# Norm sums on all partitions, router work inside the last output projection, and a first expert pair without an empty result

## The chip, the cores and the metric

The kernel runs on one core of a Trainium2 chip. The metric is the device time of one execution in microseconds (us), taken as the median of several runs. TensorE (PE) multiplies matrices, VectorE (DVE) and ScalarE (ACT) do elementwise work, GpSimd (POOL) does a few small things, and SyncE (SP) starts the DMA transfers of the weights. PE's clock is granted at one of two levels, 1.2 GHz (0.5 in the profile) or 2.4 GHz (1.0).

## The reference

Two layers work on 272 tokens of width 1024 (16 learned meta tokens and 256 of input). Each layer adds a mixer of two halves, latent attention with 8 heads and a gated linear recurrence, and then a feed-forward. Layer 0 has a dense one, layer 1 a mixture of eight experts, two for each token.

```python
u = rmsnorm(h, norm_mix_g[l]);  proj = u @ w_in[l]
mix = concatenate([rmsnorm(att, attn_out_g[l]), rmsnorm(rnn, rnn_out_g[l])])
h = h + mix @ w_out[l]
u = rmsnorm(h, norm_ffn_g[l])
# layer 1: mixture of experts
logits = u @ router_w;  top_val, top_idx = top_k(logits, 2);  top_w = softmax(top_val)
out = sum over e of (gates[:, e:e+1] * (silu(u @ w_g[e]) * (u @ w_u[e]))) @ w_d[e]
```

`rmsnorm(x, g)` is `x / sqrt(mean(x*x) + 1e-6) * g`.

## The kernel before

The hidden state `hT` lies with its 1024 features on partitions, as 8 chunks of 128 features by 272 tokens. Weights come over one queue of SP into a ring of four slots (`raw`). ACT copies each piece to fp32r (`whi`, L843), DVE subtracts the copy from the original (`wlo`, L1206), and PE multiplies each product three times (`matmul3`, L585 to L587: high by high, low by high, high by low). The rings `whi` and `wlo` have four slots, so ACT can copy piece s only when PE is done with piece s-4. All four engines run their own instruction streams in the order written and meet at semaphores. The eight PSUM banks are handed out by `plan_blocks`; `filled` counts blocks that PE has finished, and `emptied` counts for each bank how often its reader is done.

**Norms.** For the first norm of a layer (`n1ss`), `sums` (L1745) adds the squares into one row of 272. ACT takes the root of that row into `rr` (`root_rows`, L875, followed by a tiny `mark`, L811), DVE takes the reciprocal (`rows`, L1218), PE spreads the row over 128 partitions (`spread`, L1750, block `n1bc`), and ACT copies the result to `rsb` (L855). DVE then scales every block of the input projection by `rsb` (L1264). The norm of the recurrence (`rnss`, `rnbc`) goes the same way, except that DVE reads the spread sums from PSUM (`rn_scaled`, L1418). In PE's order `rnbc` stands after the turned attention output of tile 1 (L1954) and ahead of the values of tile 2 (L1930, L1943), and both `rnbc` and that output use bank 4.

**Last output projection (layer 1).** PE first does the recurrence's half (12 matmuls a block) of blocks 0 to 3 while the attention ends. Then it turns the last attention tile (L1954), ACT writes its high part (L1015), DVE its low part (L1409), and PE does the attention half of blocks 0 to 3 (12 matmuls each) and all 24 matmuls of blocks 4 to 7. For each block DVE adds to `hT` (L1476) and writes `u32`, which is `hT` by the gain (L1481), and ACT squares `hT` into `qT` (L865).

**Router.** PE then adds the squares of the tokens by 16 matmuls with one moving column (L1998, block `n2ss`), computes the logits by 16 matmuls with eight moving columns (L2059, `lg`), and turns `u32` (blocks `ut`) and `hT` (blocks `ht`), each 16 chunks, to tokens on partitions (L2069). DVE scales the logits, picks the best two (L1565 to L1570), asks ACT for an exponential (L1097), and works out `sel` and `gate` in a chain of small operations (L1572 to L1584). ACT and DVE write the tokens as high and low parts, `uhi` (L1103) and `ulo` (L1593). PE counts the places of the tokens (`cum`, L2076 to L2080), DVE writes one-hot matrices for the first pair of experts (`hot`, L1621), and PE gathers the pair's tokens by multiplying with them (L2107, 16 matmuls of the high and 16 of the low part), which ACT copies to `xeh` and `xel` (L1117).

**Experts.** `expert` handles one expert: `hidden` (L2149) in 16 pieces, `turn` (L2161), `down` (L2174) in 8. The result of an expert is copied out of PSUM at the start of the next (`result`: L1123, L1641), scattered back by `combine` (L2122, L2123), and added to `acc` by `add_expert` (L1635). The first expert thus combines an empty result: `onehT` and column 0 of `gate` are zero. A loop takes six experts as three pairs, and the last two are written out.

Of the kernel before, what the change touches and what calls it, by code (L numbers as in the profile page):

```python
# [138 lines left out]
class Chain:  # L139
# [11 lines left out]
    def loop(self, times, per):  # L151
        start = self.base + self.n
        with self.eng.Fori(0, times) as i:
# [22 lines left out]
              ("out", 1), ("rnbc", None), ("values", 2), ("out", 2)],  # L176
             [("scores", 1), ("scores", 2), ("values", 1), ("rnss", None), ("out", 1), ("rnbc", None), ("values", 2),
# [8 lines left out]
def plan_blocks():  # L186
# [6 lines left out]
    for l in range(DEPTH):  # L193
        def add(*name, bank=None):
            pl.add((l, *name), bank)
        for k, (n, c) in enumerate(IN_BLOCKS[:N_IN - CH]):
# [3 lines left out]
            if k == 2:  # L200
                add("n1bc", bank=4)
# [38 lines left out]
        for m in range(KD):  # L240
            add("wo", m)
        if l == 0:
            for j, b in enumerate((0, 1, 2, 3)):
                pl.add(("ff0", j), b)
            pl.loop("ff", [4, 5, 6, 7, 0, 1, 2, 3], 5)
            pl.loop("dn", [4, 5, 6, 7], 2)

        else:
            add("n2ss", bank=4)
            pl.add("lg", 0)  # L250
            for n in ("ut", "ht"):
                for t in range(2):
                    for hf in range(2):
                        pl.add((n, t, hf))
            pl.add("cum", 4)
# [33 lines left out]
for _l in range(DEPTH):  # L289
    for _name in ["n1", "lat", "qk", "rnn"]:  # L290
# [4 lines left out]
def build(nc, ins, out):  # L295
# [4 lines left out]
    with ExitStack() as ctx:  # L300
# [92 lines left out]
        lgt = sb("lgt", [P, 2, NE], to=moe)  # L393
        top = sb("top", [P, 2, 8], to=moe)
# [70 lines left out]
        n2_root = sem("n2_root")  # L465
        qscale_done = sem("qscale_done")
# [18 lines left out]
        topx = sem("topx")  # L485
        sel_done = sem("sel_done")
# [226 lines left out]
        def _(pool):  # L713
# [63 lines left out]
            for l in range(DEPTH):  # L777
# [18 lines left out]
                if l:  # L796
                    power(rv[:, 3:5])
# [5 lines left out]
        def _(act):  # L803
# [63 lines left out]
            def broadcast(b):  # L867

                take(b, rsb[:, :])
                mark().then_inc(rsb_done, 1)  # L870
# [38 lines left out]
            for l in range(DEPTH):  # L909
# [6 lines left out]
                root_rows(B[l, "n1ss"], 1)  # L916
                for k, (name, c) in enumerate(IN_BLOCKS[:N_IN - CH]):
                    if k == 2:
                        broadcast(B[l, "n1bc"])
# [104 lines left out]
                for k0, t in enumerate(tl):  # L1024
# [16 lines left out]
                    if t == 2:  # L1041
                        root_rows(B[l, "rnss"], 1)
# [55 lines left out]
            for t in range(2):  # L1098
                for hf in range(2):
                    b = B["ut", t, hf]  # L1100
                    act.wait_ge(filled, b.ready())
                    act.wait_ge(rstd_done, POWERS[1, "n2"])
                    act.activation(uhi[:, :, :].rearrange("p k t -> p (k t)")[:, t * D + hf * 512:t * D + hf * 512 + 512],  # L1103
                                   ps[:, b.bank, :], ACT.Copy, scale=rv[:, t + 3:t + 4]).then_inc(tok_hi, 1)
            for t in range(2):
                for hf in range(2):
                    take(B["ht", t, hf], acc[:, t, hf * 512:hf * 512 + 512], cols=slice(0, 512))

            def experts(p):
                e0 = NE * p  # L1110
                base = [(XB[b] * NE + 2) * p for b in range(2)]
# [13 lines left out]
                def expert(e, gathers, more):  # L1125
# [16 lines left out]
                    result(used)  # L1142
                    w(e, p, 3, 4, 5, 6)
                    sigmoid(0, HALF_A // 2)
                    w(e, p, 7, 8, 9, 10, 11, 12, 13, 14)
# [21 lines left out]
                with act.Fori(0, PAIRS - 1) as i:  # L1167
                    expert(2 * i, None, True)
                    expert(2 * i + 1, i + 1, True)
# [17 lines left out]
        def _(dve):  # L1187
# [62 lines left out]
            for l in range(DEPTH):  # L1250
# [3 lines left out]
                rows(l, "n1", 1)  # L1254
# [159 lines left out]
                def rn_scaled(cs):  # L1414
                    b = B[l, "rnbc"]
                    dve.wait_ge(filled, b.ready())
                    for c in cs:
                        dve.scalar_tensor_tensor(tb[:, c, c0:T], xc[:, c, c0:T], col("rnn_out_g", l, c),  # L1418
                                                 bank(b, cols=slice(c0, T)), ALU.mult, ALU.mult).then_inc(rg_done, 1)
# [36 lines left out]
                rows(l, "rnn", 1)  # L1456
                normed(1)
                out_low(1)
                for h in range(0, NH, 2):
# [3 lines left out]
                    if h == 2:  # L1463
                        dve.engine_nop().then_inc(emptied[B[l, "rnbc"].bank], 1)
# [83 lines left out]
            w(0, 0, 0, 1, 2)  # L1548
# [711 lines left out]
```

## Time and profile before

| | us |
|---|---|
| median of 3 runs | 1068.51 |
| lowest, highest | 1061.14, 1069.38 |
| the profiled execution | 1068.87 |
| its span in the trace | 1067.1 |

The profiled execution lies 1.8 us above its span, which is time outside the first and last recorded instruction. Times in rows are us from the start of the span. The first number of a row is where the piece starts, the second how long it is.

### The profile page before, as it was taken

How to read it: one execution, taken by the hardware profiler on the slowest of the kernel's cores; microseconds unless marked ns; L12 is line 12 of the kernel's file. 1: busy time of each engine (PE TensorE's matmuls, PEld its weight loads, DVE VectorE, ACT ScalarE, POOL GpSimd, SP SyncE). 2: the span in 40 equal slices, each digit the busy share in tenths (PEclk: the TensorE clock that was granted, in tenths of full speed). 3: DMA queues.
4: the chain of work that ended last, by engine and by line, in shares of the span. 5: the costliest groups of instructions: out<-in, count | busy, mean ns of one | idle time of the engine just before them, and what ended most of it. 6: DMA issues, size and time to landing. Idle time of an engine off the chain costs nothing.

```text
span 1067.1 us, 15698 instructions
## 1 busy us (share of the span) xinstructions
PE 982.7 (92%) x5858; PEld 863.2 (81%) x5858; DVE 729.6 (68%) x967; ACT 573.5 (54%) x769; POOL 37.5 (4%) x67
## 2 busy tenths in 40 slices
PE   5997977999999999997967889999999999999995
PEld 3973644899999999873655889898989898989893
DVE  5554565556666555554564458897989798979893
ACT  4464053445444443453161347778777877687771
POOL 4130010000000000000000000000000000000000
PEclk9988865899999999998875969999999999999998
DMA  8401302145557673401311316998999899989971
GB/s 258 160 8 37 115 2 79 61 152 184 160 191 204 163 213 90 163 1 39 119 51 68 119 50 229 354 338 307 350 361 324 315 354 343 336 314 341 358 286 42
DMA packets 120019, 203.76 MB, mean 191 GB/s; under 512 B 5875, under 2 KB 73741, under 8 KB 119965
## 3 DMA queue, kind: packets, MB, share of 16 engines
q1 hardware_dynamic: 119504, 202.81, 55.3%
q8 instruction: 34, 0.56, 0.2%
q10 hardware_dynamic: 460, 0.23, 0.1%
q14 instruction: 21, 0.16, 0.0%
HBM read 201.98 MB, written 1.05 MB: 190 GB/s over the span
## 4 chain that ended last, share of the span: by engine, by line
PE 82%; DVE 9%; ACT 4%; issue 2%; DMA 0%; ACTq 0%; DVEq 0%; POOL 0%; POOLq 0%
PE ps L2149 20%; PE ps L585 11%; PE ps L2174 11%; PE ps L587 10%; PE ps L586 10%; PE ps L1745 3%; DVE wlo L1206 3%; PE ps L1820 2%; PE ps L2107 2%; ACT whi L843 1%; PE ps L1868 1%; PE ps L1750 1%; PE ps L1851 1%; PE ps L1943 1%; PE ps L1939 1%
## 5 line engine op out<-in xcount | busy, mean ns | idle before, releaser
L1206 DVE TENSOR_TENSOR wlo<-raw,whi 128x1536 fp32r<-128x1536 f32 (+4 forms) x296 | 437.5, 1508 | 91.7 <-ACT whi L843 89.7
L843 ACT ACTIVATE whi<-raw 128x1536 fp32r<-128x1536 f32 (+4 forms) x296 | 376.7, 1286 | 167.8 <-PE ps L587 88.2
L585 PE MATMUL ps<-uhi,whi 128*128 128x272 f32 (+1 forms) x576 | 172.6, 300 | 2.9 <-DVE ulo L1224 2.9
L587 PE MATMUL ps<-uhi,wlo 128*128 128x272 f32 (+1 forms) x576 | 170.4, 296 | 0.0
L586 PE MATMUL ps<-ulo,whi 128*128 128x272 f32 (+1 forms) x576 | 170.2, 295 | 0.0
L2149 PE MATMUL ps<-whi,xeh 128*128 128x320 f32 (+1 forms) x512 | 124.7, 325 | 0.0
L2149 PE MATMUL ps<-whi,xel 128*128 128x320 f32 (+1 forms) x512 | 123.6, 323 | 0.0
L2149 PE MATMUL ps<-wlo,xeh 128*128 128x320 f32 (+1 forms) x512 | 123.5, 323 | 0.0
L585 PEld LDWEIGHTS ps<-uhi,whi 128*128 128x128 f32 (+1 forms) x576 | 112.7, 196 | 9.6 <-issue 9.1
L586 PEld LDWEIGHTS ps<-ulo,whi 128*128 128x128 f32 (+1 forms) x576 | 113.1, 196 | 0.0
L587 PEld LDWEIGHTS ps<-uhi,wlo 128*128 128x128 f32 (+1 forms) x576 | 112.7, 196 | 0.0
L2149 PEld LDWEIGHTS ps<-whi,xeh 128*128 128x128 f32 x512 | 88.9, 188 | 1.9
L2149 PEld LDWEIGHTS ps<-whi,xel 128*128 128x128 f32 x512 | 89.1, 188 | 0.0
L2149 PEld LDWEIGHTS ps<-wlo,xeh 128*128 128x128 f32 x512 | 89.1, 188 | 0.0
L2174 PE MATMUL ps<-whi,heh 128*128 128x512 f32 x176 | 70.0, 398 | 0.0
L2174 PE MATMUL ps<-wlo,heh 128*128 128x512 f32 x176 | 69.6, 395 | 0.0
L2174 PE MATMUL ps<-whi,hel 128*128 128x512 f32 x176 | 69.5, 395 | 0.0
L587 PE MATMUL ps<-ahi,wlo 128*128 128x272 f32 x176 | 50.9, 289 | 0.0
L585 PE MATMUL ps<-ahi,whi 128*128 128x272 f32 x176 | 50.7, 288 | 0.0
L586 PE MATMUL ps<-alo,whi 128*128 128x272 f32 x176 | 50.6, 287 | 0.0
L2174 PEld LDWEIGHTS ps<-whi,hel 128*128 128x128 f32 x176 | 33.1, 188 | 8.0
L2174 PEld LDWEIGHTS ps<-whi,heh 128*128 128x128 f32 x176 | 33.1, 188 | 7.1
(285 smaller groups left out, 1393.9 us busy)
## 6 DMA issues: line engine op xcount, KB each, us to landing
raw<-in_moe_w_down_dram SPq DMA_DIRECT2D x24, 1536.0 KB, 7.7
raw<-in_moe_w_gate_dram SPq DMA_DIRECT2D x16, 1536.0 KB, 7.7
raw<-in_moe_w_up_dram SPq DMA_DIRECT2D x16, 1536.0 KB, 8.1
raw<-in_moe_w_gate_dram SPq DMA_DIRECT2D x16, 1280.0 KB, 7.0
raw<-in_moe_w_up_dram SPq DMA_DIRECT2D x16, 1280.0 KB, 6.1
raw<-in_ffn_w_gate_dram SPq DMA_DIRECT2D x11, 1024.0 KB, 5.3
raw<-in_ffn_w_up_dram SPq DMA_DIRECT2D x11, 1024.0 KB, 5.3
raw<-in_ffn_w_down_dram SPq DMA_DIRECT2D x8, 1408.0 KB, 7.0
```

What stands on the lines that cost most here:

```text
L585: pe.matmul(dst, wh, xh, start=start, stop=False, skip_group_check=True)
L586: pe.matmul(dst, wh, xl, start=False, stop=False, skip_group_check=True)
L587: return pe.matmul(dst, wl, xh, start=False, stop=stop, skip_group_check=True)
L843: act.activation(placed(whi, s, src), src, ACT.Copy).then_inc(hi_done, 1)
L1206: dve.tensor_tensor(placed(wlo, s, src), src, placed(whi, s, src).bitcast(F32), ALU.subtract).then_inc(lo_done, 1)
L1745: q = pe.matmul(ps[0:n, bk, 0:T], con[r, at:at + n], src(c)[r, :], start=(i == 0), stop=(i == len(parts) - 1))
L1750: return pe.matmul(ps[0:width, bk, 0:T], ident[0:rows, row:row + 1].to_broadcast([rows, width]), rr[0:rows, :], start=True, stop=True)
L1820: q = pe.matmul(bank(b, slice(0, QKH)), wq[:, k, h * QKH:(h + 1) * QKH], cq[:, k, :], start=(k == 0), stop=(k == QC - 1))
L1851: q = pe.matmul(bank(b, slice(0, NOPE)), wkv[:, k, at:at + NOPE], ckv[:, k, :], start=(k == 0), stop=(k == KVC - 1))
L2107: m = pe.matmul(ps[:, b, c * 2 * P:(c + 1) * 2 * P], part[:, t * D + at:t * D + at + P], onehot[:, t, :, :], start=(t == 0), stop=(t == 1))
L2149: q = pe.matmul(ps[:, 2 * kind + n, 0:width], xs[:, kk, half, :], w[:, sl, at:at + width], start=(kk == 0 and xs is xeh and w is whi), sto ...
L2174: q = pe.matmul(ps[:, 4 + n, :], xs[:, kk, :], w[:, sl, at:at + 512], start=(kk == 0 and xs is heh and w is whi), stop=(kk == FEC - 1 and ...
```

## The change

1. **Norm sums.** A new helper `total` sums with a stationary matrix of ones, so that the sum of squares stands on all 128 partitions. ACT takes its root straight into `rsb` (for `n1`) or `rr` (for `rnn`), and DVE takes the reciprocal there. The blocks `n1bc` and `rnbc` with their spread matmuls are gone, and so is ACT's copy to `rsb`.
2. **Last output projection of layer 1.** Its blocks use three banks in turn, with the recurrence's half of three blocks (0 to 2) done ahead, not of four. After block m, PE runs `chosen(m-1)`: one matmul of the logits with the router weights stationary and 256 tokens moving, and the two turns of `u32` for that chunk. POOL adds the squares of chunks 1 to 6 to chunk 0, so that `n2ss` takes 4 matmuls. The logits stand on 8 partitions: ACT copies them, and PE turns them by two small transposes.
3. **Router.** The best two are picked from logits that are not scaled. `sel` comes from one comparison and one addition, the exponential and `gate` come later, in the first expert (`shares`). ACT copies weight piece 0 ahead of `uhi` and pieces 1 and 2 behind it. DVE takes the low part of piece 0 ahead of `pos` and `hot`, writes `ulo` behind `hot`, and takes pieces 1 and 2 after that.
4. **First expert.** It has no `result`, no `combine` and no `add_expert`. The turns of `hT` and their copies to `acc` are done inside it instead. The first pair is written out in front of the loop, which now takes two pairs.

```diff
-                root_rows(B[l, "n1ss"], 1)
+                root_all(B[l, "n1ss"], rsb[:, :], D, n1_root)
-                    if k == 2:
-                        broadcast(B[l, "n1bc"])
...
+            def root_all(b, dst, n, done):
+                act.wait_ge(filled, b.ready())
+                act.activation(dst, bank(b), ACT.Sqrt, bias=eps[:, :], scale=1.0 / n).then_inc(emptied[b.bank], 1)
+                act.wait_ge(emptied[b.bank], b.before + 1)
+                mark().then_inc(done, 1)
...
+            def total(bk, src, n):
+                for c in range(n):
+                    q = pe.matmul(ps[:, bk, 0:T], ones(slice(0, P), P), src[:, c, :], start=(c == 0), stop=(c == n - 1))
+                return q
...
 # POOL
                 if l:
+                    for m in range(1, KD - 1):
+                        pool.wait_ge(nsq_done, 3 * KD + m + 1)
+                        pool.tensor_tensor(qT[:, 0, NMETA:T], qT[:, 0, NMETA:T], qT[:, m, NMETA:T], ALU.add)\
+                            .then_inc(nsum_done, 1)
+                        pool.wait_ge(nsum_done, m)
                     power(rv[:, 3:5])
...
 # PE, last projection and router
-                halves = range(4)
+                halves = range(4 if l == 0 else 3)
+                def chosen(c):
+                    b = B["lgT"]
+                    pe.wait_ge(u_done, c + 1)
+                    q = pe.matmul(ps[0:NE, b.bank, 0:SEQ], rw[:, c, :], u32[:, c, NMETA:T], start=(c == 0), stop=(c == KD - 1))
+                    for t in range(2):
+                        b = B["ut", t, c // 4]
+                        lead, n = TILES[t + 1]
+                        q = pe.transpose(ps[:, b.bank, c % 4 * P:c % 4 * P + P], u32[:, c, lead:lead + n], ident)
...
+                    if l and m:
+                        chosen(m - 1)
+                    chosen(KD - 1)
+                        for c in (0, KD - 1):
+                            q = pe.matmul(ps[:, b.bank, t:t + 1], qT[:, c, lead:lead + n], one[:, :], start=(c == 0),
+                                          stop=(c == KD - 1))
+                    for t in range(2):
+                        q = pe.transpose(ps[:, b.bank, t * NE:(t + 1) * NE], rr[0:NE, t * P:(t + 1) * P], ident[0:NE, 0:NE])
...
 # ACT
-            w(0, 0, 0, 1, 2)
-            act.wait_ge(top_done, 1)
-            act.activation(rtmp[:, 1, 0:2], rtmp[:, 0, 0:2], ACT.Exp).then_inc(topx, 1)
+            act.activation(rr[0:NE, 0:SEQ], ps[0:NE, b.bank, 0:SEQ], ACT.Copy).then_inc(emptied[b.bank], 1)
+            mark().then_inc(lgs_done, 1)
+            w(0, 0, 0)
...             # the four uhi (L1103)
+            w(0, 0, 1, 2)
...
                     w(e, p, 3, 4, 5, 6)
                     sigmoid(0, HALF_A // 2)
+                    if first and not p:
+                        act.activation(rtmp[:, 1, 0:2], rtmp[:, 0, 0:2], ACT.Exp).then_inc(topx, 1)
+                        for t in range(2):
+                            for hf in range(2):
+                                take(B["ht", t, hf], acc[:, t, hf * 512:hf * 512 + 512], cols=slice(0, 512))
...
 # DVE
+            link(dve.tensor_tensor(pick[:, :, :, :], e8, chosen, ALU.is_equal))
+            dve.tensor_tensor(sel[:, :, 0:NE], pick[:, :, 0, :], pick[:, :, 1, :], ALU.add).then_inc(sel_done, 1)
+            w(0, 0, 0)
...             # pos, hot(0, 0), the four ulo (L1593)
+            w(0, 0, 1, 2)
...
-                    result((NE + 1) * p + e + 1)
+                    if not first:
+                        result(NE * p + e)
                     w(e, p, 3, 4, 5, 6)
                     silu(0, HALF_A // 2)
+                    if first and not p:
+                        shares()
+                    if not first:
+                        add_expert(0, [n0[0] + 1, n0[1] + 1], e)
...
 # every engine
-                    expert(2 * i, 0, i, None)
-                    expert(2 * i + 1, 1, i, i + 1)
+                expert(0, 0, 0, None, True)
+                expert(1, 1, 0, 1)
+                with pe.Fori(0, PAIRS - 2) as i:
+                    expert(2 * i + 2, 0, i + 1, None)
+                    expert(2 * i + 3, 1, i + 1, i + 2)
```

## Rows read from the trace of the kernel before

**Rows 1.** The page, part 1: busy time of each engine over the span.

```profile
PE 982.7 (92%) x5858; PEld 863.2 (81%) x5858; DVE 729.6 (68%) x967; ACT 573.5 (54%) x769; POOL 37.5 (4%) x67
```

**Rows 2.** The chain that ended last, 590 to 712 us: start, length, what.

```profile
593.73 0.39 PE ps L585
...
610.98 0.13 PE ps L587
...
612.12 6.22 PE ps L1998 x32
618.34 6.85 PE ps L2059 x32
...
630.62 1.31 PE ps L2069 x8
...
636.38 5.54 PE ps L2107 x32
641.92 8.36 PE ps L2149 x48
650.28 0.23 PE ps L2122
```

**Rows 3.** Windows: busy time of PE, PEld, DVE, ACT, POOL; PE clock; DMA share; GB/s.

```profile
612.00:613.00 1.00, 0.88 (x8) 0.88 (x8) 0.00 (x0) 1.00 (x2) 0.00 (x0) 1.00 0.00 0
...
638.00:639.00 1.00, 1.00 (x7) 1.00 (x6) 0.00 (x0) 0.71 (x2) 0.00 (x0) 0.50 0.00 0
```

**Rows 4.** Timeline, recurrence norm, layer 1; in brackets idle time before, and releaser.

```profile
570.00 1.13 DVE L1409 SCALAR_TENSOR_TENSOR mx<-ps,vec,mx 128x128 fp32r<-128x128 f32 x4 [2.07 <-ACT mx L1015]
...
571.17 1.27 PE L1750 MATMUL ps<-rr,con 1*128 1x272 f32 x2 [2.47 <-DVE mx L1409]
...
573.10 0.42 DVE L1369 COPY pT<-ps 128x256 f32<-128x256 f32 x1 [1.98 <-PE ps L1930]
```

**Rows 5.** Timeline, the same place in layer 0.

```profile
178.50 0.42 DVE L1369 COPY pT<-ps 128x256 f32<-128x256 f32 x1 [1.98 <-PE ps L1930]
```

**Rows 6.** Timeline of PE around the spread of the first norm, layer 0.

```profile
33.14 0.72 PE L1750 MATMUL ps<-rr,con 1*128 1x272 f32 x2
33.79 0.39 PE L585 MATMUL ps<-uhi,whi 128*128 128x272 f32 x1
```

**Rows 7.** Timeline of DVE, last projection and router.

```profile
586.96 0.49 DVE L1392 TENSOR_SCALAR osb<-osb,rv 128x512 f32<-128x512 f32 x1 [0.73 <-POOL rv L755]
...
595.45 0.42 DVE L1476 TENSOR_TENSOR hT<-hT,ps 128x256 f32<-128x256 f32 x1 [1.79 <-PE ps L587]
...
613.48 5.09 DVE L1206 TENSOR_TENSOR wlo<-raw,whi 128x1536 fp32r<-128x1536 f32 x3 [1.52 <-ACT whi L843]
...
625.80 0.23 DVE L1565 MAX8 top<-lgt 128x8 f32<-128x8 f32 x2
...
635.12 1.11 DVE L1621 TENSOR_SCALAR onehot<-con,pos,sel 128x128 fp32r<-128x128 f32 x4
```

**Rows 8.** Timeline of ACT, router.

```profile
616.21 1.28 ACT L1097 ACT_TABLE_LOAD   x1
...
628.73 0.69 ACT L1103 ACTIVATE uhi<-ps,rv 128x512 fp32r<-128x512 f32 x1 [0.17 <-PE ps L2069]
...
631.31 2.57 ACT L855 ACTIVATE acc<-ps 128x512 f32<-128x512 f32 x4 [1.04 <-PE ps L2069]
```

**Rows 9.** Timeline of POOL: one operation at 22 us, and one in layer 1.

```profile
22.40 1.74 POOL L739 TENSOR_SCALAR rope<-rope 32x272 f32<-32x272 f32 x1
...
503.69 1.80 POOL L786 TENSOR_TENSOR vt<-vt,con 128x512 f32<-128x512 f32 x1 [40.34 <-ACT vt L855]
```

**Rows 10.** Timeline of PE, sums of squares in layer 1's first norm.

```profile
424.52 3.83 PE L1745 MATMUL ps<-u,con 128*1 128x272 f32 x16
```

**Rows 11.** Windows of two experts, number 4 in the loop, number 6 behind it.

```profile
848.12:898.09 49.97, 49.61 (x281) 45.95 (x280) 46.50 (x39) 36.46 (x32) 0.00 (x0) 1.00 0.95 353
...
951.21:1001.17 49.96, 49.60 (x280) 45.93 (x280) 46.44 (x39) 36.38 (x32) 0.00 (x0) 1.00 0.95 354
```

More of the change, by code:

```diff
@@ L240, in plan_blocks @@
         for m in range(KD):
-            add("wo", m)
+            add("wo", m, bank=None if l == 0 else m % 3)
+            if l and m == 4:
+                pl.add(("ut", 0, 0), 4)
+                pl.add(("ut", 1, 0), 6)
         if l == 0:
@@ L248, in plan_blocks @@
         else:
[L249 to L255, printed above, removed]
+            pl.add("lgT", 3)
+            pl.add(("ut", 0, 1), 5)
+            pl.add(("ut", 1, 1), 7)
+            add("n2ss", bank=2)
+            pl.add("lg", 3)
+            pl.add("cum", 3)
+            for t in range(2):
+                for hf in range(2):
+                    pl.add(("ht", t, hf), 4 + 2 * t + hf)
     return pl
@@ L289 @@
 for _l in range(DEPTH):
-    for _name in ["n1", "lat", "qk", "rnn"]:
+    for _name in ["lat", "qk"]:
         ROWS_DONE[_l, _name] = len(ROWS_DONE) + 1
@@ L1253, in _ @@
                     mix(l, 2, 3)
-                rows(l, "n1", 1)
+                dve.wait_ge(n1_root, l + 1)
+                dve.reciprocal(rsb[:, :], rsb[:, :]).then_inc(rsb_done, 1)
                 dve.wait_ge(rsb_done, 2 * l + 1)
@@ new lines, in _ @@
+            dve.wait_ge(emptied[b.bank], b.before + 1)
+            for t in range(2):
+                q = dve.max(top[:, t, :], lgt[:, t, :])
+            link(q)
+            for t in range(2):
+                q = dve.max_index(topi[:, t, :], top[:, t, :], lgt[:, t, :])
+            link(q)
+            link(dve.tensor_copy(topf[:, :, 0:2], topi[:, :, 0:2]))
+            e8 = con[:, C_E8:C_E8 + NE].rearrange("p (a b e) -> p a b e", a=1, b=1).to_broadcast([P, 2, 2, NE])
+            chosen = topf[:, :, 0:2].rearrange("p t (j o) -> p t j o", o=1).to_broadcast([P, 2, 2, NE])
@@ new lines, in _ @@
+            dve.wait_ge(sel_done, 1)
+            hot(0, 0)
+            for hf in range(2):
+                for t in range(2):
+                    b = B["ut", t, hf]
+                    dve.wait_ge(tok_hi, 2 * hf + t + 1)
+                    v = slice(t * D + hf * 512, t * D + hf * 512 + 512)
+                    dve.scalar_tensor_tensor(ulo[:, :, :].rearrange("p k t -> p (k t)")[:, v], ps[:, b.bank, :],
+                                             rv[:, t + 3:t + 4], uhi[:, :, :].rearrange("p k t -> p (k t)")[:, v].bitcast(F32),
+                                             ALU.mult, ALU.subtract)\
+                       .then_inc(emptied[b.bank], 1)
@@ L2017, in group @@
                                 pe.wait_ge(nsq_done, 2 * KD)
-                                for c in range(KD):
-                                    q = pe.matmul(ps[:, 4, 0:T], one[:, :].to_broadcast([P, P]), u32[:, c, :],
-                                                  start=(c == 0), stop=(c == KD - 1))
-                                q.then_inc(n2_filled, 1)
+                                total(4, u32, KD).then_inc(n2_filled, 1)
                     group([0, 1, 2, 3], FFS0, 0, 0, [B["ff0", q].before for q in range(4)])
@@ L2124, in combine, with expert @@
                           .then_inc(xr_full[hf], 1)
-                def expert(e, half, pair, gathers):
+                def expert(e, half, pair, gathers, first=False):
                     n0 = [base[b] + XB[b] * e for b in range(2)]
```

263 lines of the change are left out of this document (117 added, 146 removed).

## The prediction, written before the changed kernel was run

> **What bounds the kernel now.** I read the page first: PE is busy for 92% of the span and nothing else comes near [rows 1]. So the time is PE's work plus the places where PE waits or runs at half clock, and a change pays only where it takes instructions off PE or shortens a chain that PE waits for. I then read the chain of waits from 590 us on. From the start of the attention half of the last projection (593.73) to the first expert matmul behind the gather (641.92) it passes 48.2 us [rows 2]. Some 17.4 us of that are the projection itself. After it come 6.2 us for 16 matmuls that move one column each, 6.9 us for 16 that move eight, a chain of small DVE operations that ends near 629.8, and 5.5 us of gather. The clock is 1.0 at 612, where 8 instructions of the one-column matmuls take 0.88 us [rows 3]. All 32 take 6.22 us [rows 2], 0.19 each and not 0.11, so most of them ran at half clock, and so did the gather at 638 [rows 3]. The experts are PE at full clock, 50.0 us for expert 4 in the loop and 50.0 for expert 6 written out [rows 11].
>
> **The norms.** The spread of the first norm stands between two matmuls of a stage in which PE never pauses. From its start to the next matmul is 33.79 - 33.14 = 0.65 us [rows 6]. Twice (two layers) that is 1.3 us gone. The sums, the root and the reciprocal keep their column count of 272, and a stationary matrix of 128 columns in place of one costs PE nothing in a stream that is paid by moving columns, so I take 0 for them. The earlier `rsb` frees DVE, which was not the limit there.
>
> The recurrence norm is worth more, because its spread stood behind a wait. PE waited for DVE's low part (570.00 + 1.13), because both blocks use bank 4, then spread for 1.27 us, and only then turned the probabilities that DVE copied from 573.10 on [rows 4]. DVE sat idle for 1.98 us for that. After the change PE turns them during the wait, and DVE copies as soon as its low part is written, at 571.17. That is 1.93 us, and layer 0 shows the same idle 1.98 [rows 5]. From there to the projection PE's queue is the limit, so both gains reach it: 3.9 us. The root and reciprocal are off this path in both kernels, since they come ahead of the attention output on DVE. The bounds are 0 and 4.
>
> **Last projection.** With three blocks ahead instead of four, PE reaches the turn of the last attention tile 12 matmuls sooner. These run at 0.118 us (144 matmuls from 593.73 to 611.1 [rows 2], with the first one slower), so 1.42 us. DVE had the tile ready at 587.45 [rows 7], so the start moves from 593.73 to 592.3, and the 12 matmuls are paid back behind it. Net 0. The stage is then 156 x 0.118 = 18.4 us.
>
> Into it go seven `chosen`. A sum of 8 fp32 matmuls with 272 columns takes 3.83 us at full clock [rows 10], so one with 256 takes 0.43. Eight turns take 1.31 us [rows 2], so two take 0.33. Seven times 0.76 is 5.3 us, and the last block leaves PE at 592.3 + 18.4 + 5.3 = 616.0, against 611.1 before. PE never waits for `u32` in this, if DVE keeps its pace: an addition of 0.42 and a scaling of 0.35 [rows 7] behind each block, and a low part of 1.2 for four of them, against 1.42 + 0.76 = 2.2 us of PE for the shortest block.
>
> POOL's six additions are new here. The nearest row is 1.80 us for 512 columns [rows 9], so 0.9 for 256. Behind a block of 3.6 us each they are done before PE asks. A POOL operation took 1.74 us at 22 us on 32 partitions while DVE was subtracting [rows 9], so the two can hold each other up. I charge 0.3 us, with bounds of 0 and 2 (two full additions in DVE's way during the short blocks). The Trainium skill gives a reason (SBUF — State Buffer, "SBUF: two separate sides"): VectorE and GpSimd share a port pair under an exclusive lock, and a VectorE operation with two SBUF inputs and a GpSimd one shut each other out for a whole instruction. By that rule each of the six could hold DVE for its full 0.9 us. The sum would be at most 1 to 2 us later, since only the three short blocks lack slack, and it lies inside the bounds.
>
> **Router.** The chain after 616.0, step by step: `u32` of the last chunk, 0.2; `chosen(7)`, 0.76; 4 one-column matmuls at 0.22 (8 instructions in 0.88 us [rows 3]), 0.9; two small transposes, 0.2, so 618.1. ACT's copy of the logits (0.4 and a `mark` of 0.2) hides behind the one-column matmuls. DVE's copy, maximum, index, cast, comparison and addition are six steps of 0.2 to 0.4 [rows 7], 1.65 in all: `sel` at 619.8. The five products of `cum` take 1.1 us at full clock or 2.2 at half. Beside them DVE takes the low part of piece 0, a third of 5.09 = 1.70 [rows 7], to 621.5. Then two small operations and `hot`, 1.11 [rows 7], with latencies 1.7: gather at 623.3. That is 13.1 us ahead of the 636.38 of before [rows 2]. The gather took 5.54 at a mix of clocks. PE has been nearly idle since 618, so I take half clock throughout: 32 x 0.208 = 6.7, to 630.0. The `uhi` are ready: POOL's power ends near 619.0, four at 0.69 [rows 8] end at 621.9, weight pieces 1 and 2 at 624.8, and ACT then follows the gather. `ulo` (four, 2.7 us behind `hot`) ends at 626.0, before the low gather at 626.7. So the first expert matmul comes at 630.0 instead of 641.92. I take 11.9, less POOL's 0.3: 11.6 us. With the gather at full clock it would be 1.8 more; with a wait for `ulo`, pieces 1 and 2 or ACT, 2 less.
>
> **First expert.** PE loses four pairs of `combine` matmuls: eight at 0.23 [rows 2] = 1.8. It gains 16 turns of `hT`, two times 1.31 [rows 2] = 2.6. That is 0.8 us longer. ACT loses a copy of 1.06 and gains 2.57 for `acc` [rows 8], and a table load of 1.28 [rows 8] that stood in idle time moves to just ahead of the first tanh. The copies would end near 643, weight piece 7 has its low part near 646, and PE asks for it near 647.2. So about 1 us of slack, and I take 0; if it fails, up to 3 us. The Trainium skill charges more for the load (ScalarE: Activation LUTs, "What ACT_TABLE_LOAD costs"): about 2.66 us with the drain. By the page the slack would be gone and some 0.4 us lost. No row here shows the drain apart from the 1.28.
>
> **Peeling.** Experts inside and behind the loop take 49.97 and 49.96 us [rows 11]. So the branch was free and its removal gains nothing. Price 0.
>
> **The sum.** 1.3 + 3.9 + 11.6 - 0.8 = 16.0. The profiled execution is 1068.87 (1.8 above its span), and the median is 1068.51, 0.4 below it. 1068.9 - 16.0 = 1052.9; I say **1053.0**.
>
> **Rivals.** *A, the forecast*: the terms hold within their bounds, and the time is 1049 to 1057. *B, a new wait in the first expert or in the gather*: pieces 1 to 3, the copies to `acc` or the tanh come late. For it: weight work of 5.1 us stood in a gap of the router and now stands on the queues that feed the gather, and slack is 1 us. Against it: PE needs 6.3 us for the first three pieces. Price 3 to 6 us, so 1056 to 1059. *C, a better clock*: the router's PE work no longer spans 13 us of one- and eight-column matmuls, so the clock may not fall before the gather. That gives back 1.8 in the gather and 1.1 in `cum`, and perhaps 4 more in the attention, where PE also runs at half clock (1.27 us for the spread in layer 1, 0.72 in the input projection [rows 4, 6]); 1045 to 1050. Against it: PE still pauses for `sel` and `hot`, and before the change the gather ran at half clock too [rows 3]. *D, the norms give nothing*, because something else is late next (ACT's turned probabilities, or the clock): 1053 + 5.2 = 1058. Against it: DVE's idle time is put down to PE in both layers. *E, slower*: the small fp32 matmuls and transposes in the projection make the clock fall there. Then 156 matmuls go at 0.21 instead of 0.118, 14.8 us more, and the seven `chosen` double, 5.3 more. 20 against 16 gained gives 1057 for half of the stage, and 1073 for all of it; it turns the sign from 80% of the stage on. Against it: fp32 sums of 3.8 us inside layer 1's input projection ran at pitches of full clock [rows 10], and `chosen` is 0.76 in 3.6.
>
> **Chances.** A 0.58, B 0.17, C 0.13, D 0.08, E 0.04 (0.02 of it slower than before). The measurement tells about 1% (10.7 us) from no change. Faster than 1057.8 are A, C, some 0.6 of B and half of D: 0.58 + 0.13 + 0.10 + 0.03 = 0.84. Within 1% are the rest of B and D and most of E: 0.14. Slower by over 1%: 0.02. For the range, the low side takes in most of C (a full-clock gather, norms at their bound): 1046. The high side takes in B and D: 1060.
>
> **What would show it.** In the trace after: no L1750 for the first norm and PE's input projection 0.65 us shorter; DVE's first copy of tile 2 right behind its low part, without 2 us idle; a projection of some 23.7 us at clock 1.0; from its end to the first gather 7 us instead of 25; the gather at half clock, 6.7 us; expert 0 near 50.8 us and the others 50.0. A POOL addition beside a long DVE operation would show the shared hold-up, and a gap ahead of piece 7 in the first expert would be rival B. The prediction is wrong if the clock row falls to 0.5 inside the projection, or if the gather waits for ACT or `ulo` by more than 2 us.

## The result, and the profile after

| | before | after |
|---|---|---|
| median of 4 runs each, us | 1066.6 (1061.14 to 1069.38) | 1051.84 (1048.39 to 1053.29) |
| profiled execution, us | 1068.87 | 1048.39 |
| its span, us | 1067.1 | 1046.5 |
| mean granted clock of TensorE in it | 0.925 | 0.938 |

The ratio is 0.985, with an interval of 0.9821 to 0.9879: faster by 1.5%, where 1053.0 us (0.9855 of 1068.51) was forecast. The profiled execution of after is its fastest and that of before is near its slowest, so the two spans lie 20.6 us apart and the medians 14.8. A later set of runs on another chip gave after 0.9836 (0.9815 to 0.9857), so the change is worth some 15 to 17.5 us.

The page of after, part 1, and the clock row of its part 2 (each digit a slice of 26 us):

```profile
PE 964.2 (92%) x5804; PEld 853.2 (82%) x5804; DVE 725.9 (69%) x951; ACT 570.4 (55%) x766; POOL 45.3 (4%) x73
...
PEclk9998875899999999998885989999999999999997
```

PE is still the bound, at 92% as in [rows 1], with 18.5 us less work. POOL has 7.8 us more. Next, the chain of waits of after from the last projection on (start, length, what), which answers to [rows 2]:

```profile
581.08 1.13 DVE mx L1433 x4
582.29 0.38 PE ps L594
...
585.40 0.53 PE ps L2016 x2
585.93 0.37 PE ps L2024 x2
...
606.43 0.53 PE ps L2016 x2
606.96 0.37 PE ps L2024 x2
...
608.31 0.79 PE ps L2055 x8
609.10 0.24 PE ps L2062 x2
609.36 0.19 DVE lgt L1588
...
610.68 0.18 DVE sel L1601
610.86 1.67 DVE wlo L1229
...
612.81 1.04 DVE onehot L1575 x4
613.85 0.14 issue
613.98 6.23 PE ps L2154 x32
620.22 8.57 PE ps L2196 x48
628.79 1.75 PE ps L2133 x16
```

The pairs L2016 and L2024 are `chosen`, 0.90 us each, which ride between the blocks. From DVE's last low part of the attention (ends 582.21) to the first expert matmul (620.22) are 38.0 us. Before it was 593.73 to 641.92, 48.2 [rows 2]. Behind the projection DVE sits on the chain with small operations and one long low part (L1229); ACT and POOL don't appear.

The clock, in windows of after (busy time of PE, PEld, DVE, ACT, POOL; PE clock; DMA share; GB/s), for [rows 3]:

```profile
608.00:609.00 1.00, 1.00 (x10) 1.00 (x10) 0.00 (x0) 0.97 (x3) 0.00 (x0) 1.00 0.00 0
612.00:613.00 1.00, 0.26 (x3) 0.17 (x2) 0.97 (x5) 1.00 (x3) 0.00 (x0) 0.59 0.00 0
616.00:617.00 1.00, 1.00 (x7) 1.00 (x6) 1.00 (x2) 0.68 (x2) 0.00 (x0) 0.50 0.00 0
619.00:620.00 1.00, 1.00 (x11) 1.00 (x9) 1.00 (x3) 0.89 (x3) 0.00 (x0) 1.00 0.58 59
```

The projection and the norm's few one-column matmuls run at 2.4 GHz. The clock falls to 1.2 GHz at 612.2, in the middle of the router, as PE ends `cum` (611.00 to 612.26). It had paused for `sel` before that (1.69 us); its pause for `hot` (1.72 us) only follows. The clock is back at 619.0, before the first expert. Before, the router had 20.5 us at half clock (613.0 to 630.1 and 636.9 to 640.3); now it has 6.8.

The path from PE's last projection matmul to the first expert took 30.8 us before (611.12 to 641.92) and takes 12.9 now (607.33 to 620.22), with 6.3 us of `chosen` moved into the projection. These lines of the chain before go with [rows 2]:

```profile
625.41 0.36 DVE lgt L1561 x2
...
629.54 0.24 DVE gate L1584
...
629.83 0.74 DVE ulo L1593
...
633.25 0.12 PE ps L2076 x2
```

Step by step, the one-column sums went from 6.22 to 0.79 us, DVE's chain from the logits to `sel` and `gate` from 4.6 (625.19 to 629.8) to 1.5, the turns of `hT` and the `ulo` ahead of them (3.4 us, to 633.25) left the path, and so did 0.9 us of waiting for `u32` and the squares. On the other side the eight `chosen` take 7.2 us where the logits took 6.85, the small turns of the logits 0.24, and the gather 6.23 for 5.54. The stretch with `cum`, `pos` and `hot` is 3.1 us in both.

The recurrence norm of layer 1, timeline of DVE, for [rows 4]:

```profile
562.96 1.12 DVE L1433 SCALAR_TENSOR_TENSOR mx<-ps,vec,mx 128x128 fp32r<-128x128 f32 x4 [2.35 <-ACT mx L1029]
564.00 0.41 DVE L1393 COPY pT<-ps 128x256 f32<-128x256 f32 x1
```

The copy stands right behind the low part, with no bracket of idle time, where [rows 4, 5] showed 1.98 us.

So the 20.6 us between the two spans split like this. DVE's last low part starts 11.45 us earlier (at 581.08, and at 592.53 in the trace of before). The stretch from there to the first expert is 10.2 us shorter. From the first expert to the end of the span it is 1.1 us *longer* (1046.5 - 620.22 = 426.3, for 1067.1 - 641.92 = 425.2). The first part was forecast as 5.2 + 1.4, the second as 10.2 net, the third as 0.8. The first and the third needed experiments.

### The profile page after: what moved, and what is told of

Same layout as the page of the kernel before. It is cut to its first block, busy times and chain, and to the rows that moved or that the text cites. A ratio compares the mean times of both kernels' runs of the same rounds, so it can differ in the third digit from the quotient of the medians.

```text
span 1046.5 us, 15371 instructions
## 1 busy us (share of the span) xinstructions
PE 964.2 (92%) x5804; PEld 853.2 (82%) x5804; DVE 725.9 (69%) x951; ACT 570.4 (55%) x766; POOL 45.3 (4%) x73
## 4 chain that ended last, share of the span: by engine, by line
PE 82%; DVE 9%; ACT 4%; issue 2%; DMA 0%; ACTq 0%; POOL 0%; DVEq 0%; POOLq 0%
PE ps L2196 20%; PE ps L594 11%; PE ps L2221 11%; PE ps L596 11%; PE ps L595 10%; DVE wlo L1229 3%; PE ps L1857 2%; PE ps L1781 2%; PE ps L1787 2%; PE ps L2154 2%; ACT whi L857 1%; PE ps L1905 1%; PE ps L1888 1%; PE ps L1980 1%; PE ps L1792 1%
## 5 line engine op out<-in xcount | busy, mean ns | idle before, releaser
L1229 DVE TENSOR_TENSOR wlo<-raw,whi 128x1536 fp32r<-128x1536 f32 (+4 forms) x296 | 437.4, 1505 | 98.1 <-ACT whi L857 95.9
L2221 PEld LDWEIGHTS ps<-wlo,heh 128*128 128x128 f32 x176 | 33.1, 188 | 7.3
```

Source lines behind the costliest of these rows:

```text
L1229: dve.tensor_tensor(placed(wlo, s, src), src, placed(whi, s, src).bitcast(F32), ALU.subtract).then_inc(lo_done, 1)
L2221: q = pe.matmul(ps[:, 4 + n, :], xs[:, kk, :], w[:, sl, at:at + 512], start=(kk == 0 and xs is heh and w is whi), stop=(kk == FEC - 1 and ...
```

## The experiments

Ratios are to the kernel before on the same chip, whose medians were 1067.1 to 1068.5.

**1. The norms alone** (before plus part 1 of the change):

```diff
-                root_rows(B[l, "n1ss"], 1)
+                root_all(B[l, "n1ss"], rsb[:, :], D, n1_root)
...
-                        root_rows(B[l, "rnss"], 1)
+                        root_all(B[l, "rnss"], rr[:, :], DH2, rn_root)
...             # L1750 of n1bc and rnbc goes, sums become total
```

> The kernel before with part 1 of the change alone: both norm sums on all partitions, no spread matmul, nothing else. Theory (as predicted): 0.65 us less in each input projection and 1.93 us less in each attention, 5.2 us in all, so about 1061.5 beside a before of 1066.6; in the trace DVE's first copy of tile 2 comes right behind its low part, and the two places shift by these amounts. Rival (clock): between the two profiled executions 8.1 us had gone by the start of the second layer's last attention tile, not 5.2, and the half-clock time ahead of the router fell from 136 to 113 us; if the norms bring a better clock by themselves, this run gains 8 us or more. Rival (something else is late next): 2 us or less.

Measured: 1059.04 us, 0.9919 (0.9902 to 0.9935), some 8.7 us less and not 5.2. The stage from the first norm's sums to the latent's took 44.72 - 23.02 = 21.70 us for 22.80 before: 1.1 per layer, where 0.65 was forecast. Part of the rest is the clock. Ahead of the router's first one-column matmul this kernel had 123 us at half clock, and the kernel before 130 (not the 136 of the expectation), which is worth up to 3.4 us. So I took the norms apart.

**2. The first norm alone**

```diff
+                root_all(B[l, "n1ss"], rsb[:, :], D, n1_root)     # rnss and rnbc as before
```

> Before plus the first norm's sums on all partitions alone. All norm changes together gave 9 us where the prediction's sum had 5.2. Theory A (the prediction's sizes and the clock): the removed spread gives 1.1 us in each layer, 2.3 in all, as the stage did in the run with both norms; about 1066 beside a before of 1068.3. Theory B (the extra of the 9 us sits here, because the attention behind it meets another pattern of clock): 4 us or more, 1064 or less, and the half-clock time ahead of the last projection falls by more than 3 us.

Measured: 1060.17 us, 0.9937 (0.9918 to 0.9957), 6.7 us less: theory B by its size. Windows of before (columns as above), and then of this kernel:

```profile
55.00:65.00 10.00, 9.07 (x36) 7.71 (x37) 9.00 (x18) 5.58 (x8) 4.63 (x11) 0.66 0.00 0
95.00:105.00 10.00, 10.00 (x25) 3.92 (x24) 7.72 (x17) 1.32 (x3) 1.48 (x1) 0.83 0.00 0
...
452.00:464.00 12.00, 10.71 (x65) 9.79 (x65) 9.98 (x17) 2.84 (x3) 0.53 (x1) 0.86 0.00 1
```

```profile
55.00:65.00 10.00, 10.00 (x49) 8.27 (x48) 9.68 (x19) 5.92 (x11) 5.97 (x11) 0.83 0.00 0
95.00:105.00 10.00, 9.93 (x33) 3.81 (x31) 6.32 (x13) 4.18 (x5) 3.00 (x1) 1.00 0.20 67
...
452.00:464.00 12.00, 11.37 (x59) 8.94 (x60) 11.22 (x23) 4.72 (x11) 0.53 (x1) 1.00 0.00 0
```

In each of the three places 3.4 us of half clock are gone (0.17 of 10 us in the clock's column is 1.7 us lost, which is 3.4 us at half). DVE's last low part starts at 585.57 for 592.53, 7.0 earlier. With the same instructions of both traces laid side by side, PE gains 1.3 and 1.1 us in the norm's own stages and 1.6, 0.3 and 1.0 at the three places. At the second the 1.5 us gained in one group (L1868, 5.42 us for 6.89) are mostly lost ahead of it, where the half-clock stretch from 83 to 90 us now covers more of PE's work. The other 1.7 us come bit by bit, at 122 to 142 and 488 to 532 us, as other stretches fall on other work.

One pair of profiles would be thin, since the places move (experiment 11). But the mean granted clock is known for every execution: 0.934 in all five of this kernel, and 0.9287 on average in the 15 of the kernel before beside them (0.925 to 0.936). That is 12 us less of half clock. So the better clock is real; which stretch goes is not told by it. The profiled execution, the fastest of the five, also had 13.7 us of half clock in its router for 20.5, which belongs to its whole gain of 11.1 us and not to the norm's stages.

**3. The recurrence norm alone**

```diff
+                        root_all(B[l, "rnss"], rr[:, :], DH2, rn_root)     # n1ss and n1bc as before
```

> Before plus the recurrence norm's change alone. Theory A: DVE's 1.98 us of idle time goes in each layer and nothing more, 3.9 us: 1064.5 beside a before of 1068.3. Theory B (the spread of one row at half clock also pulled the clock down around it): 6 us or more, 1062 or less, with less half-clock time in the attention than before; the two runs then sum to the 9 us of both norms together.

Measured: 1062.9 us, 0.996 (0.9949 to 0.9972), 4.2 us less: theory A's size. Its way there is not as simple. In layer 0 the wait gave 1.1 us up to DVE's last low part (196.56 for 197.68) and a half-clock stretch of 3.4 us behind it (200 to 204) went as well. In layer 1 the wait itself gave 2.0 us, and the last low part came 5.95 us earlier in all. But the profiled execution has 3.4 us of half clock in the projection (589 to 593) that before did not have, and a gather of 6.02 us for 5.54. Over all ten executions the mean granted clock is that of before (0.9281 for 0.9287), so the 4.2 us are not a better clock on average. The sum of the two single parts is 6.7 + 4.2 = 10.9, both together give 8.7. The intervals are 2.1, 1.2 and 1.8 us to either side, so the difference of 2.2 is within the noise.

**4. The router's part alone** (after with both norms as before)

```diff
-                root_all(B[l, "n1ss"], rsb[:, :], D, n1_root)
+                root_rows(B[l, "n1ss"], 1)
...
-                        root_all(B[l, "rnss"], rr[:, :], DH2, rn_root)
+                        root_rows(B[l, "rnss"], 1)
```

> After with both norms as they were before. Theory A (the parts add): both norms gave 9.1 us beside the kernel before, so this takes 9 more than after, about 1060.5, and 7 to 8 less than before. Theory B (the parts don't add, the clock of the attention is the same in whatever kernel and the norms' extra belongs to chance): 5.2 more than after, 1056.5. By the prediction's own terms it would be 10.8 less than before, 1057.5; with the 2.6 us that the experts lose to the moved buffers, 1060.

Measured: 1061.38 us, 0.9942 (0.9922 to 0.9962), 6.2 us less than before and 9.5 more than after by the medians of two chips. Within the intervals the parts add: 8.7 and 6.2 make 14.9, and the whole change gave 14.8 by its medians and 16.0 by its ratio. The time between DVE's last two low parts fell from 22.53 to 21.14 us. That is 1.39 for the start that was forecast 1.42 earlier. So the norms gave more than their price, and the larger part of the change less: 6.2 for 10.8.

**5. Riding, or only cheaper instructions?** (after, the eight `chosen` behind the projection)

```diff
-                    if l and m:
-                        chosen(m - 1)
...
-                    chosen(KD - 1)
+                    for c in range(KD):
+                        chosen(c)
```

> The changed kernel with all eight pieces of router work (logits and turns of u32) behind the last output projection, not between its blocks; same instructions, other place. Theory A (PE's instruction time counts and the place doesn't, since PE is busy in the projection anyway): the same time within 1 us, since 7 x 0.76 us leaves the projection and comes back behind it; the wait for the last chunk of u32, some 0.4 us, may be added. Theory B (riding in the projection hides the work): 4 to 5.5 us slower than the changed kernel. The clock may fall later or sooner in the router; its row will tell.

Measured: 1050.21 us, 0.9839 (0.9819 to 0.9859), as after. From the low part's end to the first expert 38.02 us passed, for 38.01. So where the pieces stand is worth nothing: PE does them one after the other in either place, and no wait was covered. Their new form did not pay either, as far as the traces show. The eight pieces are 8 x 0.90 = 7.2 us at clock 1.0, of which the logits are 8 x 0.53 = 4.2. Before, 16 matmuls of eight columns took 6.85 us at half clock [rows 2]; 16 of one column took 3.80 in experiment 6, nearly all at 1.0. So the old logits at full clock would take 3.4 to 3.8 us (an estimate: half of 6.85, or that row), no more than the new. The 16 turns of `u32` took 3.67 us at half clock then, beside DVE's chain and off the path. What shortened the path are the other steps listed above.

**6. POOL's six additions away** (after, the sums of squares in 16 one-column matmuls again)

```diff
-                        for c in (0, KD - 1):
+                        for c in range(KD):
...             # POOL's loop over m and PE's wait for it go
```

> The changed kernel without POOL's six additions; PE adds the squares of all eight chunks with 16 one-column matmuls, as before the change. Theory: 12 more such matmuls at 0.12 us each with the full clock still held (8 instructions, 4 matmuls, took 0.88 us in the kernel before, 0.79 after) is 2.6 us more on the path; if the clock falls in them, as it did before the change, 4.5 us or more. DVE's operations in the short blocks get faster, worth 0 to 0.5. Rival (POOL holds DVE up enough to matter): the same time or faster.

Measured: 1054.28 us, 0.9864 (0.9844 to 0.9885), 1.5 us more than after by its 0.985, and 3.0 by the 0.9836 of experiment 11. The intervals of these ratios overlap, so the trace has to decide. The chain of this kernel:

```profile
611.29 3.80 PE ps L2049 x32
...
617.08 0.57 PE ps L2111 x2
617.65 0.43 PE ps L2112 x2
...
620.94 5.55 PE ps L2148 x32
```

The one-column matmuls take 3.80 us for 0.79. They run at clock 1.0 up to 614.3, but then it falls, with no pause of PE ahead of it, and it is down when `cum` comes: 0.43 a pair, where after has the five pairs in 1.26 us. The stretch from low part to first expert is 42.6 us for 39.2 in experiment 11 and 39.3 in experiment 7, which have the same 3.4 us of half clock in the projection. So it is 3.3 more: 3.0 for the matmuls themselves and 0.3 for `cum` at half clock. The gather is no slower (5.55 for 5.53).

**7. The buffer `pick` moved behind all others** (after; it stood in the middle and shifts what lies behind it by 128 bytes on each partition)

```diff
-        pick = sb("pick", [P, 2, 2, NE], to=moe)
...
         ylo = sb("ylo", [P, D], F32R, to=moe)
+        pick = sb("pick", [P, 2, 2, NE], to=moe)
```

> The changed kernel with one line moved: the small buffer pick (128 bytes a partition) is laid behind all the experts' buffers and not in front of them, so that every buffer behind it (xeh, xel, heh and so on) lies at the address of the kernel before. In the changed kernel 48 matmuls of 384 columns take 8.48 us, before it took 8.34, while those of 320 and 512 columns take the same in both. Theory (address): 8.34 again, which is 0.28 us an expert and 2.3 us in all. Rival (the written-out pair, the loop's place in the code, or anything else than the address): 8.48 stays and the time is that of the changed kernel.

In after, each 48 expert matmuls with 384 columns took 8.48 us, and 8.32 to 8.34 before. Those with 320 or 512 columns were unchanged. Chain of after, second expert:

```profile
670.50 8.48 PE ps L2196 x48
...
679.90 4.24 PE ps L2196 x24
```

Chain of this kernel, the same matmuls:

```profile
672.05 8.32 PE ps L2196 x48
...
681.28 4.17 PE ps L2196 x24
```

Measured: 1048.52 us, 0.981 (0.9793 to 0.9827), 2.8 us less than after by its 0.9836 (experiment 11), with no instruction changed. The intervals of the two ratios overlap; the traces don't: the first seven experts take 359.2 us, and 361.5 in both profiles of after.

**8. The cross-check: before with an unused buffer of 128 bytes**

```diff
         lgt = sb("lgt", [P, 2, NE], to=moe)
+        pad = sb("pad", [P, 32], to=moe)
```

> The kernel before with an unused buffer of 128 bytes a partition laid where the change lays pick, and nothing else. Theory (address): its 384-column matmuls slow down from 8.34 to 8.48 us for 48, experts of 50.0 become 50.3 us, 2.3 to 2.6 us in all, so about 1070.5 beside a before of 1068.5. Rival (the address matters only together with something of the changed kernel): 8.34 stays and the time is that of the kernel before.

Measured: 1071.59 us, 1.003 (1.0019 to 1.0041), 3.2 us *slower*. Chain of this kernel:

```profile
702.74 4.24 PE ps L2150 x24
...
746.79 8.47 PE ps L2150 x48
```

The first seven experts take 361.6 us for 359.3, so 2.6 of the 3.2 us are accounted for with the eighth. An address alone is worth some 0.25% in either direction. That it is the address is shown; which of the shifted buffers matters, and why only the 384-column form, stays open.

**9. PE kept busy in the router's pauses** (after, with three fp32 matmuls of 256 columns into a free bank ahead of `cum`, and three ahead of the gather; their result is not used)

```diff
...
+            def busy(n):
+                for _ in range(n):
+                    pe.matmul(ps[:, 0, 0:SEQ], ident, hT[:, 0, NMETA:T], start=True, stop=True)
...
+            busy(3)
             b = B["cum"]
...
+            busy(3)
```

> The changed kernel with PE kept busy in the two pauses of the router: three idle fp32 matmuls of 256 columns (0.43 us each at full clock) behind the turn of the logits, and three behind cum. Their results are overwritten and read by nobody. Theory: the clock fell at 612.4 in the changed kernel because PE stood still for 1.7 us ahead of cum and 1.7 us behind it; with the pauses filled it holds, cum and the gather run at full clock and the gather takes 4.9 us and not 6.2, so 1.3 to 1.5 us are gained and the half-clock time of the router (6.8 us) goes to 0. Rival (the pauses don't decide, or the fillers delay cum and hot): same time or up to 1 us slower.

Measured: 1049.92 us, 0.9834 (0.9817 to 0.985). No window of the router is below 1.0 now, and the stretch is 37.8 us for 39.2 in a run of after with the same half-clock stretch in the projection. The 1.4 us of the trace don't stand out in the ratio. Which of the two pauses matters was not tried; in after the clock fell just before the second one began.

**10. The two together: `pick` last, PE kept busy**

> Both: pick laid last, and PE kept busy in the router's two pauses. If both theories hold their gains add: about 2.3 + 1.4 us below the changed kernel, so near 1048. If the fillers don't keep the clock, the time of pick_last, 1048.5 beside a before of 1068.5.

Measured: 1045.47 us, 0.9785 (0.9768 to 0.9803). This beats both kernels, 23.0 us below before by its ratio and 5 to 6 below after. The two gains would add to 3.7, and the rest is within the intervals. Timeline of PE in its router:

```profile
610.93 1.56 PE L2117 MATMUL ps<-hT,con 128*128 128x256 f32 x6
...
613.78 1.54 PE L2117 MATMUL ps<-hT,con 128*128 128x256 f32 x6
615.65 2.12 PE L2163 MATMUL ps<-onehot,uhi 128*128 128x256 f32 x16 [0.33 <-DVE onehot L1575]
618.22 2.15 PE L2163 MATMUL ps<-onehot,ulo 128*128 128x256 f32 x16 [0.45 <-DVEq L1620]
```

The gather takes 2.12 and 2.15 us and not 6.23 in all. But the pieces now wait 0.33 for `hot` and 0.45 for `ulo`. With PE twice as fast, DVE's `ulo` is what is late next, so of about 2 us in the gather some 1.5 reach the first expert.

**11. After once more, beside 8 to 10**

> The changed kernel itself beside the other three, as their common measure. Every theory: 1050 to 1053, with the half-clock time of its traces between 130 and 145 us; by the theory that the attention's clock windows fall by chance, its three stages ahead of the router will show another total of half-clock time than the first trace did (113 us), and the span will move with half of that difference.

Measured: 1051.38 us, 0.9836 (0.9815 to 0.9857). Its profiled execution had 39.2 us between low part and first expert, for 38.0, because 3.4 us of half clock lay in the projection (582.6 to 586.1). Ahead of DVE's last low part it had 116 us of half clock for 113, and in all 136 for 131. The same kernel places these stretches differently from one execution to the next. One that lies on PE's work all along costs half its length, 1.7 us, and less where PE would have waited.

## Why the prediction held, step by step

**The total** was right (1053.0 for 1051.84), the forecast case A, but partly because errors cancelled: the norms gave 3.5 us more than their term, and the router and experts 4.6 less by experiment 4. That the two misses were of nearly one size is luck.

**First norm: mechanism right, size too small.** The term was 1.3; its own stages gave 2.5, and the clock some 4.5 more in the profiled execution when it stands alone. The 0.65 counted from the spread's start to the next matmul. It left out that the stream on either side of the two short matmuls was broken too: from the matmul ahead of the spread to the next start it is 0.21 us, and behind the spread 0.23, where neighbours in the stream start 0.125 apart. So the spread cost 0.85. Another 0.3 went where the stream meets the sums, which themselves ran 3.67 us in place of 3.76. The clock term was named in rival C ("perhaps 4 more in the attention") and given to a case of 0.13, with no price in the sum.

**Recurrence norm: the mechanism is right, the close size partly luck.** 3.9 forecast, 4.2 measured (experiment 3). Between DVE's low part and its copy the idle time is gone in both layers, as the step said. But in layer 0 only 1.1 of the 1.98 us reached the last low part of the layer, since more of PE's work then stood at half clock. From DVE's second to its last low part of layer 1 it was 2.8 us and not 1.93, with some clock.

**Last projection: start right, `chosen` too cheap.** The start came 1.39 earlier for 1.42. Each `chosen` took 0.90 (0.53 + 0.37) and not 0.76, so seven cost 6.3 us for 5.3. The 0.43 for the logits matmul had been scaled from a sum of eight with one stationary matrix [rows 10]. What makes the single one dearer wasn't taken apart; with `chosen` all together behind the projection (experiment 5) they took 0.53 as well. PE never waited for `u32`, and the clock stayed at 1.0 in the first profile of after: rival E did not come. In the second one (experiment 11) the clock was at 0.5 for the projection's first 3 us. That was the prediction's own sign of being wrong, but the kernels of experiments 1 and 3 show the same stretch there (585.3 to 588.7 and 589.2 to 592.6) without any `chosen`, so it is not E's mechanism. E's own sum has a slip: half of 20 us on 1053 is 1063, not 1057.

**POOL: a hold-up, but on POOL's side.** Timeline of POOL in after:

```profile
587.31 1.54 POOL L808 TENSOR_TENSOR qT<-qT 128x256 f32<-128x256 f32 x1 [9.82 <-ACT qT L879]
589.33 1.40 POOL L808 TENSOR_TENSOR qT<-qT 128x256 f32<-128x256 f32 x1 [0.48 <-ACT qT L879]
593.07 1.41 POOL L808 TENSOR_TENSOR qT<-qT 128x256 f32<-128x256 f32 x1 [2.34 <-ACT qT L879]
596.31 0.73 POOL L808 TENSOR_TENSOR qT<-qT 128x256 f32<-128x256 f32 x1 [1.83 <-ACT qT L879]
```

And of DVE, its low parts there:

```profile
587.03 1.22 DVE L1229 TENSOR_TENSOR wlo<-raw,whi 128x1024 fp32r<-128x1024 f32 x1
...
588.92 1.22 DVE L1229 TENSOR_TENSOR wlo<-raw,whi 128x1024 fp32r<-128x1024 f32 x1
...
592.66 1.23 DVE L1229 TENSOR_TENSOR wlo<-raw,whi 128x1024 fp32r<-128x1024 f32 x1 [0.34 <-ACT whi L857]
```

Three additions beside DVE's low parts took 1.40 to 1.54 us, and three without one 0.73 to 0.74. DVE's low parts of 1024 elements stayed at 1.22 to 1.23, and one scaling took 0.38 for 0.35. So the charge of 0.3 should have been near nothing. Each time DVE had started first, and POOL's addition ended 0.6 us after DVE's low part. By the Trainium skill (SBUF — State Buffer, "SBUF: two separate sides") whichever of the two starts first holds the shared port pair for its whole instruction and the other waits. The trace agrees with that. That DVE is held by POOL is not seen here, since POOL never came first.

**Router: a little shorter than its steps.** From the projection's last block (607.33) to the first expert 12.9 us passed, for 14.0. The gather had clock 1.0 again from 619.0 on (6.23 for 6.7), and `cum` was still at full clock (five pairs in 1.26 us). With `chosen` 1.0 dearer, the two nearly cancel: 38.0 us for the stretch, and the forecast's was 37.7 to 38.0. That the experiment's medians give only 6.2 for this part has one cause that is shown, the experts' 2.6 (below), and one that is likely: a half-clock stretch at the start of the projection, up to 1.7, that most of the profiled executions have and the first ones of before and after have not. How often the unprofiled ones have it isn't known.

**First expert: the turns were too dear, an address was missed.** The 16 turns of `hT` took 1.75 us for 2.6: the row of 1.31 for eight [rows 2] was not a price for them. The clock was 1.0 there too (by the windows from 631 to 633), so it wasn't the clock; why they ran at 0.16 each there and at 0.11 here is not settled. With 1.8 of `combine` gone, this would be a change of 0. But the expert took 670.50 - 620.22 = 50.28 for 49.97 [rows 11], and all that follow it are 0.3 longer too (a window of an expert in the loop, 723.95 to 774.24, is 50.29; those that also gather for the next pair take 53.45 for 53.12). This is the step that failed: "experts the others 50.0". The prediction costed instructions and not buffers, and 8 x 0.32 = 2.6 us came from one new buffer of 128 bytes (experiments 7 and 8). From the first expert to the end the trace shows only 1.1 more, because the last expert and what follows took 65.0 us for 66.1; why stays open. The table load took 1.28, and the tanh followed at 629.57:

```profile
628.27 1.28 ACT L1145 ACT_TABLE_LOAD   x1
629.57 0.81 ACT L1145 ACTIVATE sg<-ps 128x768 f32<-128x768 f32 x1
```

So the 2.66 us with a drain, which the Trainium skill states (ScalarE: Activation LUTs, "What ACT_TABLE_LOAD costs"), are not seen: the tanh starts 0.02 us behind the load, and the load 0.01 us behind ACT's copy (626.77 + 1.49). PE had no gap ahead of piece 7: rival B did not come.

**Peeling: 0, not tried by itself.** In after the experts in the loop and written out took the same time to 0.02 us, which fits; no run isolates it.

**What stays open.** How the first norm's spread, two short matmuls at 33 us, bears on the clock of what follows. That the clock is better without it is shown over all executions of experiment 2; which stretches go is not. Of the 6.8 us at 57 us one half was also gone in experiments 4 and 8, which have the spread. The stretch at 97 was gone in experiments 1, 2, 7, 9 and 10, and that at 459 in experiments 2 and 5 and in the first profile of after; its second profile had both. So the clock term of a single part is known only on average, here some 3 to 5 us.

## What to carry to other kernels

Price a removed instruction by the two neighbours whose pitch it breaks, and in a kernel bound by PE add a term for the granted clock: list its stretches in the profile, and ask of each small matmul and each pause in front of one what it does to it; judge it by the mean clock of many executions, not by two traces. Matmuls that move one column are paid by their count: twelve fewer gave 3.0 us at nearly full clock (experiment 6), and sixteen of them took 6.22 us in place of 3.80 where the clock had fallen. A matmul with 256 moving columns in place of two with eight was no cheaper at the same clock (by the estimate in experiment 5), and where it stands in the order is of no matter if no wait is covered. When a change adds a buffer, compare the pitch of an untouched inner loop before and after: a shift of 128 bytes was worth a sixth to a fifth of this whole change, and putting the new buffer last gave it back.

## What was not expected of the hardware

- Expert matmuls with 384 moving fp32r columns take 8.32 to 8.34 us per 48 at one buffer address and 8.47 to 8.48 with all behind it shifted by 128 bytes per partition, at the same clock of 1.0. Forms with 320 and 512 columns don't change.
- POOL's addition of 256 columns takes 0.73 us alone and 1.40 to 1.54 beside DVE's subtraction from two SBUF operands, when the subtraction started first, and the subtraction doesn't get longer (1.22 to 1.23).
- A stretch of half clock of 3.4 us comes and goes between executions of one kernel. Without two short matmul instructions per layer (experiment 2) the mean granted clock was 0.934 for 0.9287. Six filler matmuls of 256 fp32 columns in two pauses kept the clock at 1.0 through the whole router, in both profiles taken (experiments 9 and 10).
